# A different order of attention heads in a hybrid diffusion step: neighbourhood and MLA heads alternate

## What is computed

```python
q_mla, c_kv, k_rope, na_q, na_k, na_v, gq, gk, gv = mixer_inputs(h, w_in[l], ...)
# 6 MLA heads: 64+32 wide keys; keys and values come from c_kv @ w_kv_up, the 32 rotary columns are shared
k_m, v_m = mla_keys_values(c_kv, apply_rope(k_rope), w_kv_up[l])
# 4 neighbourhood heads: latents see an 8 x 16 window (with a bias table) and all context keys
o_na = neighbourhood_attention(na_q, na_k, na_v, cache_na_k, cache_na_v, na_rpb[l])
# 6 grouped-query heads on 2 key/value heads, q and k RMS-normed and rotated
o = concat([o_mla, o_na, o_gqa], axis=-1)
x = x + g_a * (o @ w_out[l])
```

## Time and profile before

| | us |
|---|---|
| median of 3 runs | 1882.93 (1881.45 to 1883.32) |
| the profiled execution | 1889.33 |
| its span in the profile | 1887.5 |
| attention, layer 0 / layer 1 (first exponential to output weights) | 196 to 419 / 1111 to 1328 |

### The profile page before, as it was taken

How to read it: one execution, slowest core, us unless ns; L and a number is a source line. 1 busy time by engine, 2 the same in 40 slices (tenths; PEclk the granted TensorE clock), 3 DMA queues, 4 the chain that set the end, 5 groups by cost and what they waited for, 6 DMA issues and landing times.

```text
span 1887.5 us, 29279 instructions
## 1 busy us (share of the span) xinstructions
PE 1738.5 (92%) x11772; PEld 1684.5 (89%) x11772; DVE 1160.3 (61%) x2218; ACT 698.4 (37%) x1382; POOL 214.4 (11%) x314
## 2 busy tenths in 40 slices
PE   6899788889899999999989977899989999999997
PEld 6898677779899999999989966777889999999997
DVE  5997757873676777776652257788364444544444
ACT  2423755762522211222143366577253222112222
POOL 0001624320000000000010053523000000000001
PEclk9999879999899999999989988999989999999998
DMA  9573000014244343333122010000412222222201
GB/s 330 172 244 107 17 1 2 1 52 128 90 153 165 127 138 140 122 122 122 42 74 81 29 40 1 1 3 23 133 46 68 89 67 67 88 90 67 67 22 56
DMA packets 109561, 159.83 MB, mean 85 GB/s; under 512 B 5089, under 2 KB 87841, under 8 KB 109217
## 3 DMA queue, kind: packets, MB, share of 16 engines
q1 hardware_dynamic: 106672, 152.53, 24.3%
q0 software_dynamic: 640, 2.92, 0.6%
q10 hardware_dynamic: 2160, 3.23, 0.5%
HBM read 155.09 MB, written 3.57 MB: 84 GB/s over the span
## 4 chain that ended last, share of the span: by engine, by line
PE 77%; DVE 12%; ACT 4%; issue 2%; POOL 2%; DMA 2%; SPq 0%; POOLq 0%; DVEq 0%; ACTq 0%
PE ps L589 23%; PE ps L590 23%; PE ps L591 23%; DVE ps L1251 4%; PE ps L810 2%; PE ps L597 2%; DVE negmax L1456 1%; PE ps L789 1%; PE ps L653 1%; DVE K L1236 1%; DVE hT L1236 1%; PE ps L791 1%; DMA ada_n<-in_w_ada_first 1%; DMA wo_raw<-in_w_out 1%; DVE pT L1236 1%
## 5 line engine op out<-in xcount | busy, mean ns | idle before, releaser
L589 PE MATMUL ps<-hT,gw 128*128 128x320 f32 x1408 | 437.6, 311 | 6.8 <-DVE hT L1236 6.8
L590 PE MATMUL ps<-hT,gw 128*128 128x320 f32 x1408 | 437.3, 311 | 0.0
L591 PE MATMUL ps<-hT,gw 128*128 128x320 f32 x1408 | 437.2, 311 | 0.0
L1315 DVE SCALAR_TENSOR_TENSOR x<-ps,mod,x 128x320 f32<-128x320 f32 (+2 forms) x576 | 211.8, 433 | 120.1 <-PE ps L591 117.0
L589 PEld LDWEIGHTS ps<-hT,gw 128*128 128x128 f32 x1408 | 266.0, 189 | 7.3 <-issue 7.3
L590 PEld LDWEIGHTS ps<-hT,gw 128*128 128x128 f32 x1408 | 265.9, 189 | 0.0
L591 PEld LDWEIGHTS ps<-hT,gw 128*128 128x128 f32 x1408 | 265.8, 189 | 0.0
L1544 DVE TENSOR_TENSOR mm<-sl,ps 128x320 f32<-128x320 f32 x88 | 42.7, 487 | 318.1 <-issue 185.4
L589 PE MATMUL ps<-act,dw 128*128 128x320 f32 x704 | 219.3, 311 | 2.7 <-DVE act L1236 2.7
L590 PE MATMUL ps<-act,dw 128*128 128x320 f32 x704 | 219.0, 311 | 0.0
L591 PE MATMUL ps<-act,dw 128*128 128x320 f32 x704 | 218.9, 311 | 0.0
(11 more groups left out here) (201 smaller groups left out, 3644.3 us busy)
## 6 DMA issues: line engine op xcount, KB each, us to landing
gw_raw<-in_w_gate SPq DMA_DIRECT2D x22, 1024.0 KB, 5.5
gw_raw<-in_w_up SPq DMA_DIRECT2D x22, 1024.0 KB, 8.0
dw_raw<-in_w_down SPq DMA_DIRECT2D x22, 1024.0 KB, 5.0
ada_w<-in_w_adaT SPq DMA_DIRECT2D x39, 512.0 KB, 6.7
ada_wf<-in_w_adaT SPq DMA_DIRECT2D x34, 512.0 KB, 6.8
wi_raw<-in_w_in SPq DMA_DIRECT2D x16, 912.0 KB, 5.6
ada_wq<-in_w_adaT SPq DMA_DIRECT2D x19, 512.0 KB, 4.2
wo_raw<-in_w_out SPq DMA_DIRECT2D x16, 512.0 KB, 4.3
```

What stands on the lines that cost most here:

```text
L589: pe.matmul(dst, lh, rh, start=start, stop=False, skip_group_check=True)
L590: pe.matmul(dst, lh, rl, start=False, stop=False, skip_group_check=True)
L591: return pe.matmul(dst, ll, rh, start=False, stop=stop, skip_group_check=True)
L1315: i = ve.scalar_tensor_tensor(out=x[:, o, c0:c1], in0=ps[:, banks + hf_, s0:s0 + c1 - c0], scalar=mod[:, l, part * KD + o, q:q + 1], in1=x ...
```

## The change

The order of heads becomes N0 N1 | M0 N2 | M1 N3 | M2 M3 | M4 M5 | G0 ... G5 (bars between pairs). The first MLA preparation (M0) therefore falls into N1's slots instead of N3's. Pairs of two kinds make their values per head: an MLA head in a mixed pair computes Va/Vb for itself alone (`values_of`), and every neighbourhood and grouped-query head has a "V" entry of its own. The rotated key columns are written when a key buffer changes from another kind to MLA (`fresh`): for M0 (head 2) and M3 (head 7). The key rotations KR come before the first scores, the query rotations QR in the first four slots, WK in slot 3 instead of 6. BM of N2 and N3 move from slots 5 and 10 to 10 and 20. The rows of `w_out` are laid out on the host in the order of the pairs. Buffer counts, banks and the number of score, transpose and value products stay; the single-head Va/Vb are 64 columns wide per tile instead of 128.

```diff
-HEADS = [("na", h) for h in range(4)] + [("mla", h) for h in range(6)] + [("gqa", h) for h in range(6)]
+HEADS = [("na", 0), ("na", 1), ("mla", 0), ("na", 2), ("mla", 1), ("na", 3), ("mla", 2), ("mla", 3), ("mla", 4), ("mla", 5)]
+HEADS += [("gqa", h) for h in range(6)]
+HEAD_ROW = {"mla": 0, "na": 384, "gqa": 640}
...
+def fresh(g):
+
+    before = [e for e in range(g) if key_slot(e)[0] == key_slot(g)[0]]
+    return not before or HEADS[before[-1]][0] != HEADS[g][0]
+
+def values_of(g):
+
+    if HEADS[g][0] != "mla":
+        return []
+    if HEADS[g ^ 1][0] != "mla":
+        return [g]
+    return [] if g % 2 else [g, g + 1]
...
         s = [("Qa", g), ("Ka", g), ("QKb", g)]
-        if h < 2:
+        if fresh(g):
             s.append(("Kpe", g))
...
-        if g % 2 == 0:
-            if HEADS[g][0] == "mla":
-                turns += [("M", "Va", g), ("M", "Vb", g)]
-            else:
-                extra[10 * g + 7].append(("V", g))
+        if values_of(g):
+            turns += [("M", "Va", g), ("M", "Vb", g)]
+        if HEADS[g][0] != "mla":
+            extra[10 * g + 7].append(("V", g))
...
-    spread([("KR", t) for t in range(4)] + [("QR", t) for t in range(4)], 0, 15)
+    spread([("QR", t) for t in range(4)], 0, 4)
     spread([("GS", t) for t in range(NT)] + [("GR",)], 8, 16)
-    spread([("WK",)], 6, 1)
+    spread([("WK",)], 3, 1)
     spread([("GZ", t) for t in range(NT)], 25, 18)
-    order = [("BM", 0)]
+    order = [("BM", 0)] + [("KR", t) for t in range(4)]
...
-                    if kind == "mla" and g == 4:
+                    if kind == "mla" and h == 0:
                         pe.wait_ge(q_roped, 8 * l + 8)
...
-                        src = [wkv[:, q, h * P:(h + 2) * P].rearrange("p (a b) -> p a b", a=2)[:, :, 64:P] for q in range(2)]
-                        m = split_mm(ps[:, 7, n * P:(n + 1) * P], ckvT[:, 0, k0:k0 + P], ckvT[:, 1, k0:k0 + P],
+                        heads = len(values_of(g))
+                        src = [wkv[:, q, h * P:(h + heads) * P].rearrange("p (a b) -> p a b", a=heads)[:, :, 64:P] for q in range(2)]
+                        m = split_mm(ps[:, 7, n * 64 * heads:(n + 1) * 64 * heads], ckvT[:, 0, k0:k0 + P], ckvT[:, 1, k0:k0 + P],
                                      src[0], src[1], True, True)
...
-                            if slot == 0 and mt == 0:
+                            if mt == 0:
-                                if kind_of_pair(pair) == "mla":
-                                    pe.wait_ge(misc_done, l * NM + MISC_AT[("Vb", 2 * pair)] + 1)
+                                if HEADS[g][0] == "mla":
+                                    pe.wait_ge(misc_done, l * NM + MISC_AT[("Vb", g if values_of(g) else g - 1)] + 1)
                                 else:
-                                    pe.wait_ge(v_ready, l * NV + v_at(pair) + 1)
-                                if pair > 0:
+                                    pe.wait_ge(v_ready, l * NV + V_AT[g] + 1)
+                                if slot == 0 and pair > 0:
                                     pe.wait_ge(o_ready, l * 2 * NP + 2 * pair - 1)
...
                         if h >= 2:
-                            po.wait_ge(max_ready, l * UNITS + 5 * (h - 1))
+                            po.wait_ge(max_ready, l * UNITS + 5 * (head_of("na", h - 2) + 1))
...
+    rows = np.zeros(DM, np.int64)
+    for n, (kind, h) in enumerate(HEADS):
+        r0 = PAIR_TILE[n // 2] * P + 64 * (n % 2)
+        rows[r0:r0 + 64] = HEAD_ROW[kind] + 64 * h + np.arange(64)
+    w_out = g["w_out"][:, rows]
```

More of the change, by code:

```diff
@@ L165, with head_of @@
 S_AT = {s: n for n, s in enumerate([s for s in SCHED if s[0] == "S"])}
[L166 to L174, removed]
+V_AT = {s[1]: n for n, s in enumerate([s for s in SCHED if s[0] == "V"])}
+NV = len(V_AT)
+C_AT = {g: n for n, g in enumerate([g for g in range(NH) if cached(g)])}
+assert len(C_AT) == 8
+def head_of(kind, h):
+    return HEADS.index((kind, h))
 def last_t_of(g):
@@ L402, in build, with v_slots @@
         block = ctx.enter_context(nc.Block())
-        def v_slots(pair, q, t0, n):
-            v = V[:, pair % 2, q, t0:t0 + n, :]
-            return bass.AP(tensor=v.tensor, offset=v.offset, ap=[list(v.ap[0]), [192, n], [128, 2], [1, 64]])
+        def v_slots(heads, q, t0, n):
+            v = V[:, heads[0] // 2 % 2, q, t0:t0 + n, 128 * (heads[0] % 2):192]
+            return bass.AP(tensor=v.tensor, offset=v.offset, ap=[list(v.ap[0]), [192, n], [128, len(heads)], [1, 64]])
         def v_sources(g, q):
             kind, h = HEADS[g]
[L412 to L421, removed]
+            pair, d0 = g // 2, 128 * (g % 2)
+            c0 = NA_V + 64 * h if kind == "na" else G_V + 64 * (h // 3)
+            cc = 64 * h if kind == "na" else 64 * (h // 3)
+            cache = vc_na if kind == "na" else vc_g
+            return [(V[:, pair % 2, q, 0:NT, d0:d0 + 64], z[:, 0:NT, c0:c0 + 64], V[:, pair % 2, 0, 0:NT, d0:d0 + 64]),
+                    (V[:, pair % 2, q, 5, d0:d0 + 64], cache[:, cc:cc + 64], V[:, pair % 2, 0, 5, d0:d0 + 64])]
         def ring_of(l, t):
@@ L642, in misc_step @@
                             m = pe.transpose(ps[0:96, 7, o0:o0 + P], qm[:, t, h * 96:(h + 1) * 96], ident[:])
-                            if what == "QKb" and h < 2:
+                            if what == "QKb" and fresh(g):
                                 m = pe.transpose(ps[0:96, 7, P:2 * P], z[:, t, OFF_KR - 64:OFF_NA], ident[:])
@@ L990, in cached_keys @@
                     sc.activation(K[:, kb, 0, LAT:640], kc_g[:, h // 3, :], ACT.Copy).then_inc(kc_hi, 1)
-                elif kind == "mla" and h < 2:
+                elif kind == "mla" and fresh(g):
                     sc.activation(K[64:96, kb, 0, LAT:640], kc_pe[64:96, :], ACT.Copy).then_inc(kc_hi, 1)
@@ L1021, in misc_hi_part @@
                     t0, n = (0, 4) if what == "Va" else (4, 2)
-                    dst = v_slots(pair, 0, t0, n)
-                    i = sc.activation(dst, ps[:, 7, 0:n * P].rearrange("p (t a b) -> p t a b", t=n, a=2), ACT.Copy)
+                    heads = values_of(g)
+                    src = ps[:, 7, 0:n * 64 * len(heads)].rearrange("p (t a b) -> p t a b", t=n, a=len(heads))
+                    i = sc.activation(v_slots(heads, 0, t0, n), src, ACT.Copy)
                 i.then_inc(misc_hi, 1)
@@ L1322, in cached_keys @@
                 gb, (kb, new_keys) = g % 2, key_slot(g)
+                if not cached(g):
+                    return
                 if kind == "na":
-                    n, src, r = g, kc_na[0:64, h, :], slice(0, 64)
-                elif kind == "gqa" and new_keys:
-                    n, src, r = 6 + kb, kc_g[0:64, h // 3, :], slice(0, 64)
-                elif kind == "mla" and h < 2:
-                    n, src, r = g, kc_pe[64:96, :], slice(64, 96)
-                else:
-                    return
-                ve.wait_ge(kc_hi, l * 8 + n + 1)
-                if kind == "gqa" or kind == "na" and h < 2:
+                    src, r = kc_na[0:64, h, :], slice(0, 64)
+                elif kind == "gqa":
+                    src, r = kc_g[0:64, h // 3, :], slice(0, 64)
+                else:
+                    src, r = kc_pe[64:96, :], slice(64, 96)
+                ve.wait_ge(kc_hi, l * 8 + C_AT[g] + 1)
+                if kind != "mla" and fresh(g):
                     ve.memset(K[64:P, kb, 1, :].bitcast(F32), 0.0)
```

26 lines of the change are left out of this document (15 added, 11 removed).

## The result

The changed kernel takes 1890.79 us (median of 5 runs, 1889.35 to 1892.82), the kernel before beside it 1882.52 (1881.03 to 1883.32): a ratio of 1.0039 [1.0028, 1.0051]. It is slower by 0.4%, 8.3 us, and the interval is clear of 1; I had forecast 2.8 us less and "no change that can be told". The time lies inside the range given, on the side of rival (a). The profiled execution of the changed kernel took 1890.79 (span 1889.0).

What follows compares the result with a forecast made beforehand. Attention steps were taken as bound by VectorE, by TensorE, or in N3 and M0 by waits on PSUM bank 7 turns. Terms -0.6 - 3.0 + 0.8 = -2.8 us gave 1880.1 from 1882.93; whole range 1866 to 1893.

Steps and rivals of the forecast that it cites:

- rival (a): Slower: clock stays half in alternating steps M0 and M1 of both layers, 3.9 us each, about 1892; chance 0.17.
- steps N0 N1 M0 N2 M1 N3 M2: Layer 1 attention, each from one head's first exponential to the next head's; sum 102.9 against 103.5 us, -0.6.
- M1: Step 5 of layer 1's attention: 8.5 us with VectorE busy and 4.5 idle, 13.0.
- M2: Step 7 of layer 1's attention: takes over old M0's six turns; VectorE 11.0 us busy and 6.8 idle, 17.8.
- M0: Step 3 of layer 1's attention: VectorE 9.7 us busy and 4.1 idle, five turns, 13.8.
- The rule that I weighed against the change: TensorE's clock is throttled by default and activity releases it, so alternating dense and thin steps runs some dense work at 1.2 GHz.
- Layer 0's -3.0: Layer 0 attention: the same -0.6 us, and 3.4 of its 5.8 surcharge for the clock left out by the change.
- rival (c): Faster: idle about 3 us in all seven steps but M2; -7.5 layer 1, -10.5 layer 0, about 1865; chance 0.23.
- The early rotations: Start of attention: key rotations cost nothing in POOL's slack; query rotations make TensorE wait about 2 us in N1, mostly covered.
- N0: Step 1 of layer 1's attention: takes in the kv weight split, loses half the value copies; 9.36 becomes 10.2 us.
- (b): Slower: PSUM bank 7 turns, 44 instead of 42 a layer, set the steps; +5 to +8, about 1888; chance 0.16.
- The last steps: End of attention: per-head grouped-query values lengthen the final step by 0 to 0.8 us; +0.4 a layer, +0.8.

Runs made afterwards that it cites:

- with the waits filled: Changed kernel plus eight idle matmuls, results unread, ahead of seven TensorE waits in each layer's attention; 1878.61 us, ratio 0.9963 to the kernel before.
- the experiment with the repairs together: Changed kernel with all rotations ahead of the scores, grouped-query values per pair, idle matmuls ahead of the waits and one N3 transpose; 1873.52 us, ratio 0.9943.

## Why the prediction was wrong, point by point

In the terms of the working, layer 1, steps N0 N1 M0 N2 M1 N3 M2: forecast 10.2, 16.0, 13.8, 15.6, 13.0, 16.5, 17.8; measured 12.0, 15.4, 10.9, 15.9, 16.0, 17.3, 21.0. The sum is off by 5.6 us (108.5 against 102.9): M1 and M2 alone are 6.2 over, the other five together 0.6 under.

- **Rival (a)'s price was left out of the steps where it fell due.** This is the step that failed: "M1: 8.5 and 4.5, 13.0" and "M2 ... 17.8" are lengths at the full clock. At that clock they came out (13.02 and 18.17 with the waits filled), M2 by luck: its load was 1.7 us too small and its idle time 1.3 too large, and M1's parts were off by half a us each way (9.05 busy and 3.97 idle, against 8.5 and 4.5). In the changed kernel both ran near 0.8. I had (a) at 0.17, with M0 and M1 as its places and the condition that both means be under 0.8. Only M1's was (0.79); M0 is full (10.90 busy of 10.95, 0.98), and the second place was M2. My argument against it was that M1 has "9 to 10 us of TensorE work at full clock in 13": a mean over the step. What decided was one wait inside it, 1.63 us in M1 and 1.73 in M2 (after M2's other, of 1.53, the clock stayed). The idle matmuls give back 6.9 us a layer, most of it in M1 and M2. The price per place, 3.9, was near: 2.7 and 3.6.
- **The rule that I weighed against the change had the right sign**, and I gave it 17 in 100; but what the runs show is not dense work next to thin work as such, since in the same order the clock stayed once the waits were filled. The Trainium skill, "TensorE: Matmul & The Clock Gate", section "A second HAM failure mode: psum-queue depth-cycling", describes a kernel where "the PE micro-idles between MM groups frequently enough that HAM oscillates" (HAM is its name for what grants the clock). These runs agree: turns of bank 7 and of the score banks, waits mostly of 1.2 to 2.7 us, and after many of them the clock at 0.50 for 3 to 10 us.
- **Layer 0's -3.0** rested on a surcharge of 5.8 that the kernel before paid in one profile and not in the other (M0 17.74 when run again). I had noted that the profiled execution stood 6.4 above the median, and yet took a gain from what made it so and put that on the median. Without it the forecast would have been about -0.4, the middle of "same". The -10.5 of rival (c) in layer 0 also counts the -0.6 twice; by its own terms it is -9.9.
- **The early rotations, costed near nothing**, are worth -3.0 and -3.5 by themselves in the old order. In the new order two of the query rotations stand between the first normalisations, as forecast, and TensorE's wait for POOL, "about 2 us", was 2.32; but it fell in N0, which is 12.0 instead of 10.2. N1 was 15.4 against 16.0, at a clock of 0.72 (14.1 with the waits filled). With all rotations first the seven steps are 2 to 4 us shorter. The error was in N0, where I moved WK and the values but not POOL's work (8.69 us busy, before 4.00).
- **M0, forecast 13.8, took 10.9.** VectorE's load was right (9.7, measured 9.5); its idle time was 1.4 instead of 4.1. Here (c) was nearer (12.6), and (b) wrong: five turns in this step cost little. The single value sets' matmuls of 64 columns start 0.11 us apart at the full clock, as far as those of 128 did, so taking "all of it" for them was right. M2's load was too small by 2 us (11.0, measured 13.0), its idle time too large (6.8; 5.5 with the waits filled).
- **N2 and N3** were within 0.8, which is luck in part: both had a fall of the clock in them (0.89 and 0.90), and N2 is 14.79 without it. The old 18.8 is gone, as listed among the signs.
- **The last steps**, +0.4 a layer: the last step grew by 0.86 (costed at 0 to 0.8), but the six grouped-query steps together did not; the term is 0. The output weights: SP issues the first at 1318.34 and ScalarE first reads them at 1330.23, 11.9 us later, where I had said some 12, and nobody waits.

```profile
1318.34 1.02 SPq L571 DMA_DIRECT2D wo_raw<-in_w_out  x2
```

```profile
1330.23 1.99 ACT L1199 ACTIVATE wo<-wo_raw 128x1024 fp32r<-128x1024 f32 x2
```

Put together, for a layer: rotations -3.3, the order +1.5 with the waits filled, the clock +6.9: +5.1, twice that 10.2 us. These are the differences between four profiled kernels, so they must add up to what the attention stretches show: 5.4 and 5.0 more in the changed kernel, profiled again, than in the kernel before, profiled again. The time shows 8.3, or 5.7 by the second ratio; what differs between the two ratios is mostly the kernel before (1882.52, then 1885.91).

The difference to 10.2 lies in a stretch that the change doesn't touch. From the output weights of layer 0 to the first exponential of layer 1 the kernel before and the two others in the old order took 690.3 to 691.1 us in four profiles, those in the new order 685.7 to 687.8 in seven and 689.7 in one: some 4 us less. The windows show the clock again, a fall that one has and the other hasn't. These stand 108 us after the start of that stretch in the kernel before and in the changed kernel, each profiled again:

```profile
520.88:523.88 3.00, 2.96 (x11) 2.96 (x12) 2.55 (x3) 1.76 (x2) 0.00 (x0) 0.50 0.79 313
```

```profile
529.01:532.01 3.00, 3.00 (x22) 3.00 (x21) 2.94 (x4) 0.98 (x2) 0.00 (x0) 1.00 0.61 242
```

Why the fall comes in one order and not in the other no experiment shows; nothing in the forecast had a term for it. With it the sum is about +6, near the 5.7; ahead of the first attention and behind the second the profiles vary by 4 and 3 us more.

Open is what the order is worth at a kept clock. With the same slots for the rotations the new order's first ten steps are 1.5 longer (143.9 against 142.3), but N3 still has a fall in them (18.58 and 18.87, against 16.95 where its wait was filled too), which is as much as the 1.5. With the rotations in front and N3's wait filled they are 140.4 to 140.8. The old order was not tried with its rotations in front.

## What to carry to other kernels

A step that is not bound by TensorE is still lengthened by TensorE's clock, if the clock falls in it: look for the waits ahead of matmuls (here mostly 1.2 to 2.7 us), and at the granted clock in the few microseconds behind each, not at the mean over the step. When work is reordered so that dense steps come to stand between thin ones, price each step at both clocks; if a wait can't be removed, idle matmuls ahead of it (not behind it) kept the clock in most cases here, worth 0.7% of the whole kernel; in the old order, where the clock mostly held anyway, they gave attention nothing. And where the one profiled execution lies apart from the median, don't count a gain on what is peculiar to it; profile it twice.

## What the runs showed of the hardware that I had not expected

**The clock fell after short waits, and not each time.** Waits of 1.20 and 1.21 us at the same place of the same program were followed by 0.50 in one layer (260 to 264 us) and by 1.00 in the other. The windows of 2 us behind the wait that ends at 255.40, and behind its twin at 1166.34:

```profile
256.00:258.00 2.00, 1.85 (x16) 1.62 (x14) 1.83 (x5) 1.23 (x3) 0.06 (x1) 1.00 0.00 0
258.00:260.00 2.00, 2.00 (x14) 2.00 (x13) 1.17 (x3) 1.65 (x4) 0.74 (x1) 0.60 0.00 0
260.00:262.00 2.00, 2.00 (x10) 2.00 (x11) 0.51 (x4) 0.73 (x3) 0.80 (x1) 0.50 0.04 8
262.00:264.00 2.00, 2.00 (x11) 1.97 (x10) 1.10 (x3) 0.27 (x2) 0.00 (x0) 0.50 0.00 0
...
1169.00:1171.00 2.00, 2.00 (x19) 1.88 (x18) 1.25 (x4) 1.64 (x4) 0.69 (x1) 1.00 0.00 0
1171.00:1173.00 2.00, 2.00 (x18) 2.00 (x18) 1.43 (x4) 1.25 (x5) 0.80 (x1) 1.00 0.00 0
```

Behind the waits looked at here the fall comes 0.4 to 3 us after the wait's end, in the middle of dense work. It is not a matter of the wait's length alone. The kernel before has a wait of 2.69 us in M2, longer than any that the changed kernel has in attention, and in layer 1 the clock stays at 1.00 behind it:

```profile
1202.32 0.66 PE L810 MATMUL ps<-ident,probs 128*128 128x128 f32 x4 [2.69 <-POOL probs L479]
```

```profile
1202.32:1205.32 3.00, 3.00 (x22) 2.85 (x23) 1.42 (x2) 1.64 (x5) 0.30 (x1) 1.00 0.00 0
```

In layer 0 of the same execution the clock fell behind its twin (292.25). The same holds for the waits of about 2 us in N3: at 1.00 when they begin, one kept the clock and one lost it. At the other end stands M1 in the experiment with the repairs together, with no wait above 0.47 us and a fall. What decides between the two is open, and so one profile doesn't tell what a wait costs: M5 was 14.75 and 14.74 in the two layers of one execution of the changed kernel and 13.17 and 13.16 in those of the other.

**A VectorE copy of two SBUF operands is slowed by POOL.** The narrow value copies (128x64) in N2 are shown in the kernel before, while POOL rotates queries without a pause (an operation of 0.98 us starts at 1141.04, one of 0.86 at 1142.10), and with the early rotations, where POOL is idle from 1130.06 to 1131.75:

```profile
1141.70 0.41 DVE L1236 TENSOR_TENSOR V<-vc_na,V 128x64 fp32r<-128x64 f32 x1
...
1142.43 0.60 DVE L1236 TENSOR_TENSOR V<-vc_na,V 128x64 fp32r<-128x64 f32 x1
```

```profile
1130.62 0.22 DVE L1236 TENSOR_TENSOR V<-vc_na,V 128x64 fp32r<-128x64 f32 x1
...
1131.16 0.22 DVE L1236 TENSOR_TENSOR V<-vc_na,V 128x64 fp32r<-128x64 f32 x1
```

0.41 and 0.60 us against 0.22, 0.57 us together; the wide copies between them hardly change (0.52 and 0.48 against 0.48 and 0.49). POOL's own operations are slower too (0.98 for one that takes 0.72 or 0.73 alone). The Trainium skill, "SBUF — State Buffer", section "SBUF: two separate sides", calls the port pair that the two engines share "an exclusive lock, not a bandwidth split"; the rows agree in direction; whether an instruction waits out a whole one of the other engine they don't show. VectorE's instructions of N2 ahead of these copies are the same in both kernels and take the same time to 0.01 us. The other half of the 1.1 us is no gain: it is a copy of queries (0.69 us) most of which falls behind the end of the step in the second kernel.
